# Attention blocks scored in fewer, wider parts, and latent heads scored over 128 rows, in a two-layer mixer kernel on Trainium2

## What is computed

```python
def diff_attention(q, k, v, lam, rel_table):            # scale = 64 ** -0.5
    ...
        s = jnp.einsum('bqhmd,bkhmd->bhmqk', qb, kf) * scale
        s = jnp.where(rel >= 0, s + bias[None, :, None], NEG)
        pm = jax.nn.softmax(s, axis=-1)
        w = pm[:, :, 0] - lam * pm[:, :, 1]
        return jnp.einsum('bhqk,bkhe->bqhe', w.astype(v.dtype), v)

def mla_attention(q_nope, q_rope, k_nope, k_rope, v):   # scale = 96 ** -0.5
    ...
        s = (jnp.einsum('bqhd,bkhd->bhqk', qn, kn)
             + jnp.einsum('bqhr,bkr->bhqk', qr, kr)) * scale
        s = jnp.where(rel >= 0, s, NEG)
        pm = jax.nn.softmax(s, axis=-1)
        return jnp.einsum('bhqk,bkhd->bqhd', pm.astype(v.dtype), v)

def sliding_window_attention(q, k, v, sinks, rel_table):  # 128 queries on 256 keys
    ...
    s = jnp.where(mask[None, :, None, None], s + bias, NEG)
    pm = jax.nn.softmax(jnp.concatenate([s, sink], axis=-1), axis=-1)[..., :-1]
    o = jnp.einsum('bnhgqk,bnkhd->bnqhgd', pm.astype(v.dtype), vb)
```

## Time and profile before

| | |
|---|---|
| time, median of 3 runs | 2990.86 us (2988.71 to 2991.18) |
| the profiled execution | 2991.07 us, of it span 2989.2 us |
| PE busy | 2949.5 us, 99% of the span |
| VectorE, ScalarE, GpSimd busy | 58%, 35%, 43% |
| attention units of the two layers, first scores to last values | 41.6 to 471 us and 667.6 to 1096 us of the span |
| TensorE clock granted | 0.992 of full speed on average |

### The profile page before, as it was taken

The page is one execution under the profiler, slowest core; times in us unless marked ns, Lnnn a source line. Parts: engine busy times, 40 slices in busy tenths (PEclk is TensorE's granted clock), DMA queues, the critical chain, the costliest instruction groups (busy, mean ns, idle before and its releaser), DMA issues.

```text
span 2989.2 us, 39167 instructions
## 1 busy us (share of the span) xinstructions
PE 2949.5 (99%) x15272; PEld 2360.9 (79%) x15272; DVE 1740.0 (58%) x3028; ACT 1055.6 (35%) x1875; POOL 1280.3 (43%) x926
## 2 busy tenths in 40 slices
PE   8999999999999999999999999999999999999999
PEld 6777777887777778788888788887888888788887
DVE  4765455475745555646553587615766666587722
ACT  4443343354343432533333322224333333432222
POOL 3333334453333345444444455544434334355543
PEclk9999999999999999999999999999999999999999
DMA  5222223232222223232222233332222222223332
GB/s 194 81 78 65 71 78 98 85 110 73 78 64 71 77 86 96 87 99 85 85 82 84 82 99 99 95 95 90 84 78 71 78 78 78 71 85 99 99 94 76
DMA packets 78332, 260.22 MB, mean 87 GB/s; under 512 B 10731, under 2 KB 13547, under 8 KB 78149
## 3 DMA queue, kind: packets, MB, share of 16 engines
q1 hardware_dynamic: 77572, 255.63, 27.6%
q10 hardware_dynamic: 576, 2.10, 0.2%
HBM read 255.53 MB, written 6.09 MB: 88 GB/s over the span
## 4 chain that ended last, share of the span: by engine, by line
PE 93%; DVE 3%; ACT 1%; DMA 1%; issue 1%; POOL 0%; SPq 0%; DVEq 0%; ACTq 0%
PE bank L714 25%; PE bank L716 25%; PE bank L715 24%; PE bank L852 2%; PE bank L899 2%; PE bank L879 1%; PE bank L731 1%; PE bank L732 1%; PE bank L738 1%; PE bank L1016 1%; PE bank L1017 1%; PE bank L1022 1%; PE bank L1111 1%; PE bank L768 1%; DMA bias_copies<-bias_vectors 1%
## 5 line engine op out<-in xcount | busy, mean ns | idle before, releaser
L565 POOL TENSOR_TENSOR w_lo<-w_raw,w_hi 128x512 fp32r<-128x512 f32 x458 | 609.8, 1332 | 1627.5 <-ACT w_hi L1250 1627.5
L714 PE MATMUL bank<-h_hi,w_hi 128*128 128x512 f32 x2367 | 944.7, 399 | 0.8 <-POOL w_lo L565 0.8
L716 PE MATMUL bank<-h_hi,w_lo 128*128 128x512 f32 x2367 | 924.6, 391 | 0.0
L715 PE MATMUL bank<-h_lo,w_hi 128*128 128x512 f32 x2367 | 923.3, 390 | 0.0
L1250 ACT CAST w_hi<-w_raw 128x1024 fp32r<-128x1024 f32 x458 | 480.1, 1050 | 1234.9 <-PE bank L716 1138.1
L567 POOL TENSOR_TENSOR w_lo<-w_raw,w_hi 128x512 fp32r<-128x512 f32 x458 | 667.3, 1457 | 35.9
L714 PEld LDWEIGHTS bank<-h_hi,w_hi 128*128 128x128 f32 x2367 | 445.4, 188 | 97.9 <-issue 9.3
L716 PEld LDWEIGHTS bank<-h_hi,w_lo 128*128 128x128 f32 x2367 | 445.1, 188 | 96.0
L715 PEld LDWEIGHTS bank<-h_lo,w_hi 128*128 128x128 f32 x2367 | 445.9, 188 | 86.4 <-issue 0.3
L2128 DVE TENSOR_SCALAR m<-bank,gains 128x512 f32<-128x512 f32 x48 | 36.1, 751 | 328.6 <-ACT ta L1453 197.0
L1388 ACT ACTIVATE probs<-probs,small_columns 128x128 f32<-128x128 f32 (+2 forms) x192 | 101.9, 531 | 168.6 <-DVE small_columns L1887 164.4
(11 more groups left out here) (321 smaller groups left out, 4473.2 us busy)
## 6 DMA issues: line engine op xcount, KB each, us to landing
w_raw<-in_w SPq DMA_DIRECT2D x458, 512.0 KB, 3.5
bias_copies<-bias_vectors SPq DMA_DIRECT2D x1, 2560.0 KB
x_res<-in_x_t ACTq DMA_DIRECT2D x4, 512.0 KB, 8.1
bias<-bias_copies SPq DMA_DIRECT2D x8, 256.0 KB, 3.3
bias<-bias_copies SPq DMA_DIRECT2D x16, 128.0 KB, 2.4
out_x<-x_res SPq DMA_DIRECT2D x8, 256.0 KB, 2.5
bias_copies<-bias_vectors SPq DMA_DIRECT2D x1, 1280.0 KB
ple_raw<-in_p_t SPq DMA_DIRECT2D x2, 512.0 KB, 3.7
```

What stands on the lines that cost most here:

```text
L565: pool.tensor_tensor(WL[slot][:, 0:half], RAW[slot][:, 0:half], WH[slot][:, 0:half].bitcast(F32), ALU.subtract).then_inc(sems["lo_half"], 1)
L714: pe.matmul(banks[bank][:], WH[slot][:, w], hi[:, k, :], start=start, stop=False)
L715: pe.matmul(banks[bank][:], WH[slot][:, w], lo[:, k, :], start=False, stop=False)
L716: pe.matmul(banks[bank][:], WL[slot][:, w], hi[:, k, :], start=False, stop=stop).then_inc(sems["kt_done"], 1)
```

## The change

Query blocks are taken in **parts** (`TOGETHER`): for differential and latent heads blocks 0 and 1 (128 + 256 columns), then 2, then 3; for window heads blocks 0 and 1 (128 + 256) and blocks 2 and 3 (256 + 256). The scores of one part lie side by side in one bank per half; they are signalled once per half, and the turn, the copy and the values of a part go together. Maxima, exponentials and probabilities are still one instruction per block and half. `cuts` gives 2 x parts + 1 places: seven shares in units 0 to 6, and in units 7 to 11 one place fewer (latent) or two fewer (window). The two buffers of probabilities alternate over parts through all units (`parity`).

For latent heads `qn` and `qr` become one tile of 128 rows per head: 64 nope, 32 rope, 32 swapped rope. The keys stand likewise: `AK` has head 0's nope keys in rows 0 to 63 and the rope keys below, `KR` the same for head 1. One score matmul per head over 128 rows replaces two over 64. For that `CS` gets ones in its upper rows once, the eviction of `qn` multiplies by `CS`, and the eviction of `kn` becomes two copies of 64 rows, with a third once a layer (unit 3) that brings the rope keys into `AK`.

```diff
+TOGETHER = {"da": ((0, 1), (2,), (3,)), "mla": ((0, 1), (2,), (3,)), "sw": ((0, 1), (2, 3))}
+def parity(n, part):
+    return (sum(n_parts(x) for x in range(n)) + part) % 2
+def placed_blocks(kind, part):
+    at_, placed = 0, []
+    for i in TOGETHER[kind][part]:
+        w = key_blocks(kind, i)[1] * P
+        placed.append((i, at_, w))
+        at_ += w
+    return placed
...
 def cuts(n):
-        places = [upto(n, round(third / 3 * (p + 1))) for p in range(3)] + [upto(n, total - BEHIND)]
+        early = max(parts - 1, 2)
+        places = [upto(n, round(third / early * (p + 1))) for p in range(parts - 1)] + [upto(n, total - BEHIND)]
...
-    share = (total - first) / 9
-    return [upto(n, round(first + share * (p + 1))) for p in range(9)]
+    share = (total - first) / (2 * parts + 1)
+    return [upto(n, round(first + share * (p + 1))) for p in range(2 * parts + 1)]
...
-                    def scores(n, i):
+                    def scores(n, part):
...
-                        for m in range(2):
-                            r = slice(64 * m, 64 * m + 64)
-                            ins = pe.matmul(banks[S0 + m][:, 0:blocks * P], AQ[r, q], keys[r, kk], start=True, stop=(kind != "mla"))
...
-                                pe.matmul(banks[S0 + m][:, 0:blocks * P], AR[r, q], KR[r, kk], start=False, stop=True).then_inc(sems["s_ready"], t.one("s_ready"))
+                        for i, at_, w in placed:
+                            kb = key_blocks(kind, i)[0]
+                            q, kk = slice(i * P, (i + 1) * P), slice(kb * P, kb * P + w)
+                            for m in range(2):
+                                r = slice(64 * m, 64 * m + 64)
+                                if kind == "mla":
+                                    ins = pe.matmul(banks[S0 + m][:, at_:at_ + w], (AQ, AR)[m][:, q], (AK, KR)[m][:, kk], start=True, stop=True)
+                                else:
+                                    ins = pe.matmul(banks[S0 + m][:, at_:at_ + w], AQ[r, q], keys[r, kk], start=True, stop=True)
+                                if i == placed[-1][0]:
+                                    ins.then_inc(sems["s_ready"], t.one("s_ready"))
...
                         dve.tensor_scalar(CS[:], CS[:], COLS[:, 1:2], None, ALU.mult).then_inc(sems["dve_step"], t.one("dve_step"))
                         dve.wait_ge(sems["dve_step"], t.at("dve_step"))
+                        dve.memset(CS[0:64, :], 1.0).then_inc(sems["dve_step"], t.one("dve_step"))
+                        dve.wait_ge(sems["dve_step"], t.at("dve_step"))
...
                         elif name == "kn":
-                            dve.tensor_copy(AK[:], bank).then_inc(sems["evicted"], 1)
+                            if n == 3:
+                                dve.tensor_copy(AK[64:128, :], KR[64:128, :]).then_inc(sems["dve_step"], t.one("dve_step"))
+                            dve.tensor_copy(AK[0:64, :], bank[0:64, :]).then_inc(sems["dve_step"], t.one("dve_step"))
+                            dve.wait_ge(sems["dve_step"], t.at("dve_step"))
+                            dve.tensor_copy(KR[0:64, :], bank[64:128, :]).then_inc(sems["evicted"], 1)
                         elif name == "qn":
-                            dve.tensor_scalar(AQ[:], bank, scale["mla"], None, ALU.mult).then_inc(sems["evicted"], 1)
+                            dve.scalar_tensor_tensor(AQ[:], bank, scale["mla"], CS[:], ALU.mult, ALU.mult).then_inc(sems["evicted"], 1)
...
-            if name == "qn":
-                return tiles(qb, np.concatenate([96 * x + np.arange(HEAD) for x in h]))
-            if name == "qr":
-                return tiles(qb, np.concatenate([96 * x + HEAD + r for x in h for r in (rope, swap)]))
+            if name in ("qn", "qr"):
+                x = h[("qn", "qr").index(name)]
+                return tiles(qb, 96 * x + np.concatenate([np.arange(HEAD), HEAD + rope, HEAD + swap]))
```

More of the change, by code:

```diff
@@ L100, in upto, with n_parts, part_width @@
     return at
+TOGETHER = {"da": ((0, 1), (2,), (3,)), "mla": ((0, 1), (2,), (3,)), "sw": ((0, 1), (2, 3))}
+def n_parts(n):
+    return len(TOGETHER[KINDS[n]])
+def parity(n, part):
[6 more added lines that the diff above has]
+        at_ += w
+    assert at_ <= SEQ
+    return placed
+def part_width(kind, part):
+    return sum(w for _, _, w in placed_blocks(kind, part))
 def cuts(n):
-    total = sum(k for _, k in ORDER[n])
+    total, parts = sum(k for _, k in ORDER[n]), n_parts(n)
     if n >= ONE_PLACE:
@@ L890, in values @@
                         pe.wait_ge(sems["pt_copied"], t.at("pt_copied", CREDITS["pt_copied"]))
[L891 to L900, removed]
+                        for i, at_, w in placed_blocks(kind, part):
+                            kb, blocks = key_blocks(kind, i)
+                            for b in range(blocks):
+                                for m in range(group(kind)):
+                                    r = slice(64 * m, 64 * m + 64)
+                                    if kind == "da":
+                                        r, p = slice(0, P), PT[parity(n, part)]
+                                        v = VT[:, kb + b, :]
+                                    else:
+                                        v, p = (CV if kind == "sw" else VT)[:, kb + b, r], PT[m]
+                                    ins = pe.matmul(banks[OUTB][r, i * P:(i + 1) * P], v, p[:, at_ + b * P:at_ + (b + 1) * P],
+                                                    start=(b == 0), stop=(b == blocks - 1))
                         ins.then_inc(sems["pv_done"], t.one("pv_done"))
@@ L917, in mix @@
                     for n in range(12):
-                        at_ = cuts(n)
-                        for i in range(QT):
+                        at_, parts = cuts(n), n_parts(n)
+                        for i in range(parts):
                             fill(n, at_[2 * i])
-                            if i + 1 < QT:
+                            if i + 1 < parts:
                                 scores(n, i + 1)
@@ L926, in mix @@
                             turn(n, i)
-                        fill(n, at_[8])
+                        fill(n, at_[2 * parts])
                         if n + 1 < 12:
                             scores(n + 1, 0)
-                        values(n, QT - 1)
+                        values(n, parts - 1)
                         if n + 1 < 8:
@@ L1423, in mix @@
                                 self.angles_out()
-                        beside(n, at_[8])
+                        beside(n, at_[2 * parts])
                         self.step = 0
@@ L1861, in mix, with maxima @@
                         dve.wait_ge(sems["gains_in"], 16)
-                    def maxima(n, i):
+                    def maxima(n, part):
                         kind = KINDS[n]
-                        w = key_blocks(kind, i)[1] * P
                         step = len(self.turns)
```

121 lines of the change are left out of this document (58 added, 63 removed).

## The result

| | before | after |
|---|---|---|
| median of 4 runs each | 2989.78 us (2987.26 to 2991.18) | 2962.57 us (2958.36 to 2964.31) |
| the profiled execution, of it span | 2991.07, 2989.2 us | 2964.31, 2962.5 us |

The ratio is 0.991, 95% interval 0.9896 to 0.9924: faster, by 22.7 to 31.1 us, where 22 were forecast. The measured 2962.57 lies 6.4 us under the forecast and 2.4 under the range. A second comparison (5 runs after, 9 before) gave 2963.35 against 2987.24, ratio 0.992 (0.9907 to 0.9934).

A forecast was written before the change was run, and what follows sets the result against it. The prediction took TensorE (PE), busy 99% of the span, as the bound; switches saved 11.0 us a layer, 22 for two, with new waits counted as 0, so 2991.07 - 22 gave 2969 us, range 2965 to 2975.

The forecast's parts named there:

- The switches: PE's attention groups: extra time beyond streaming, 0.3 to 0.55 us per half-row or half-column excursion; savings 11.0 a layer, 22 us.
- the one row that had to be chosen (0 to 0.40 for the lone latent score): Full-row latent score among projections: its switch lies between 0 and 0.40 us; taken as 0, like the turn.
- The vanished rope time: Rival, latent scores: half of 4.3 us in 8 units goes with the rope matmuls, 17 us more, 2952; chance 0.04.
- the lost pairing: Rival, differential and window units: merged half-row scores stream twice as long, 17 us back, 2986; chance 0.02.
- the exposed loads: Rival, full-row latent scores: own weight loads of 0.19 us come out of hiding, 24 us back, 2993; chance 0.02.
- The waits of the merged first part: First turn of a unit: longer chain on VectorE and ScalarE stays covered, so PE has no new wait.
- the 5.1 less 1.8 to 3.6: Unit 5's first turn: 5.1 us of cover against a chain grown by 1.8, or at most 3.6 us.
- The very first unit, counted at 0 with 1.3 less as one bound: First unit, without cover, already waiting 0.9 us: from 1.3 us less to 2 us more, taken as 0.
- There is next to no waiting to remove: PE's waits that the change could touch: two of 1.6 us together and one of 0.9 us.
- the sum's silence on the projections behind a group: The 22 us sum counted switches per attention group and no cost in the projection steps behind a group.
- The base: Starting time for the absolute forecast: profiled execution 2991.07 us, 0.2 above the median of the runs.

The follow-up runs named there:

- the first two experiments: Against the kernel before: only latent operands in 128 rows, blocks singly, 2977.75 us; only blocks taken together, latent operands as before, 2969.99 us.
- the lone half-row matmul: Changed kernel plus 24 lone half-row matmuls per layer among the projections behind the last window unit, results unused: 2998.22 us, one execution.
- the run with earlier places: Kernel before with two places of unit 3 moved ahead, after 19 and 22 tiles instead of 21 and 25: 2986.21 us, one execution.
- the lone transposes: Changed kernel plus 24 lone full-row transposes per layer among the projections behind the last window unit, results unused: 2969.43 us, one execution.
- The run with fewer places: Changed kernel with units 1 to 6 put at fewer places, as units 7 to 11 already are: 2964.15 us, ratio 0.9925.
- no rope: Kernel before without the latent heads' rope score matmuls, rotary part left out of the scores: 2971.69 us, one execution.
- the order turned round: Changed kernel with the two score loops exchanged, both blocks of one half first, then the other's: 2958.67 us in one execution, then 2962.39 us.
- on one half alone: Changed kernel with both half-row score matmuls of differential and window heads reading rows 0 to 63: 2995.95 us, one execution.

## Why the prediction was right, and where it was wrong

The change gained 27.2 us (23.9 in the second comparison) where 22 were forecast, and the time lies 2.4 us under the range. The mechanism was right, and its sum too; terms beside it were missing, and the base stood too high.

**The switches: right.** Taken group by group as in the forecast, the extra times of the two layers fell by 22.2 us without the waits, where 22 were forecast: 4.0 a layer in window units, as forecast, 5.5 in latent units with the end of unit 3 (5.4), 1.6 in differential ones (1.6). The two halves of that are seen apart in the first two experiments. The bounds of the one row that had to be chosen (0 to 0.40 for the lone latent score) were settled at 0, as taken from the earlier trace rows. The vanished rope time, the lost pairing and the exposed loads are refuted: full-row records with loads of their own follow at 0.43 (two of a head in 8.2/8 = 1.02 us, less 0.59), pairing is intact at 1.87. The Trainium skill's rule on weight loads that the forecast weighed ("TensorE: Matmul & The Clock Gate", part 3, "The mechanism") thus did not hold for these records; the page states it of packed tiles, and the same section also has a load go ahead when it targets the background weight buffer. Its page "TensorEngine Tiling (Array Packing)", "Key Properties", says that changing the tiling mode drains the engine; the 0.40 of the lone half-row matmul would fit that, the trace shows the cost and not a drain, and the page gives no figure.

**The waits of the merged first part: right, with less to spare than the terms say.** In unit 5 the last scaling of the two blocks starts at 230.68 on VectorE (the same figure as in the earlier trace rows by chance), and the turn follows on PE at 232.56 with no wait:

```profile
230.68 0.35 DVE L1937 TENSOR_SCALAR probs<-probs,small_columns 128x256 f32<-128x256 f32 x1
```

```profile
232.56 0.82 PE L909 MATMUL bank<-ident,probs 128*128 128x128 f32 x6
```

1.5 us of cover are left, the low end of the 5.1 less 1.8 to 3.6 that the forecast worked out. Counted from the projection step ahead of the unit's first scores (225.08 before, 220.54 after), the scaling ends 4.6 us later in the unit and the turn starts 2.8 later. Less the 0.7 by which that group itself got longer, the chain grew by 3.9, more than the forecast's upper bound, and a turn that came 2.1 later instead of 1.7 made up for it. That this turn does not wait is thus in part luck.

One new wait stands in unit 3 of the first layer, and not at a turn; both profiles of the changed kernel have it. A projection behind a norm's sums needs a bank that VectorE empties when it takes the rope keys out of it:

```profile
156.08 0.68 DVE L2011 TENSOR_TENSOR k_rope<-bank,rstd 128x512 f32<-128x512 f32 x1
```

```profile
156.81 0.51 PE L744 MATMUL bank<-h_hi,w_hi 128*128 128x512 f32 x1 [0.42 <-DVE k_rope L2011]
```

In VectorE's order the scalings of two blocks and the maxima of block 2 now stand ahead of it; before, VectorE came to it 1.5 us early and sat idle. With what follows from it this group is 0.6 us longer, in the second layer 0.05: 0.7 lost. That the order is the cause is read from the rows and was not tried by itself. The very first unit, counted at 0 with 1.3 less as one bound, gave 0.6 in this profile and 0.1 in the second comparison's; its waits move by as much from one execution to the next.

**The terms that were missing.** The steps that failed are "There is next to no waiting to remove" and the sum's silence on the projections behind a group.
- *The norm row's wait*, 2.0 us: the row of PE's waits between the ones that the forecast read was not costed; it stands on a line that the change does not touch. The change moves the last block's scalings ahead of the eviction that this line waits for. Shown by the run with earlier places.
- *Breaks*, 1.2 us: 98 groups a layer became 76. The projection steps between groups, those at the lower clock left out, stand 5.6 us above 0.227 each in both layers before and 4.4 after, so 44 breaks fewer gave 1.2 us, 0.03 each; that is the price of the lone transposes. The run with fewer places gives somewhat less (0.3 to 0.4 us a layer for 17 breaks, 0.02 each).

22.2, 2.0, 1.2 and 0.6, less 0.7, are 25.3, against 25.5 in the stretch; with 0.1 for the first unit 24.8, against 25.0 in the second comparison. What is left is no more than the clock moves: in both kernels there are steps of 0.43 us for some 3 us in unit 2 (below), in these profiles longer or shorter by a microsecond or so, and absent in one.

**The base.** The 2990.86 was the median of three runs; with the fourth it is 2989.78, and in four later sets of nine runs each the kernel before had medians of 2987.24 to 2988.89. That moves no gain but the absolute time, by 1 to 3.6 us of the 6.4 by which the forecast stood too high; the range reached only 4 us down. What stays open is the last 1.2 us outside the attention stretch: most of it lies between the layers, and two kernels without the change or with little of it (earlier places, no rope) have it too, so I take it for spread.

## What to carry to other kernels

On an engine that is 99% busy, cost a group by the start times around it, less its streaming: what is left tells what the form costs, and grouping work of one form pays that much per excursion saved, while putting two matmuls that ran at the same time into one pays nothing by itself, though it halves their number. When a change moves work earlier or later, go through every wait of the bound engine, also those on lines that it does not touch, and ask which queue's order they hang on. Take the base of an absolute forecast from as many runs as there are, and let the range be as wide below as above.

## What the runs showed of the hardware that I had not expected

- The two halves of the array's rows run as two streams: with the order turned round, half 1's first record started 13 ns behind half 0's, ahead of a record of half 0 that stands before it in the program, and on one half alone the same records took 0.215 us each, one by one. The Trainium skill, "TensorE: Matmul & The Clock Gate", part 3, "The mechanism", says that matmuls start and end strictly in program order; here the records' starts did not.
- A full-row transpose that interrupts a stream of projections costs 0.141 us though its own group shows 0.11, as the next three to five steps run 1 to 4% slower.
- Behind 24 one-column records of a norm's sums in unit 2 the granted clock fell to the lower level, in the profiles of both kernels. After, by stretches (start:end, length, PE busy and its records, granted clock, share of DMA, GB/s):

```profile
114.50:117.50 3.00, 3.00 (x27) 1.00 0.00 0
117.50:118.50 1.00, 1.00 (x5) 0.85 0.00 0
118.50:121.50 3.00, 3.00 (x10) 0.50 0.21 33
121.50:124.00 2.50, 2.50 (x12) 0.98 0.42 170
```

In the third stretch the clock is 0.50 of full speed (1.2 of 2.4 GHz); projection steps take 0.43 us there instead of 0.23, some 1.5 us a time. In the profile of the kernel with the latent change alone the same 24 records ran in 2.69 us of extra time, as here, and the clock stayed at 1.00 in both layers. So what makes it fall is not settled by these runs.
